# One of four combinations of the down weights on GpSimd instead of VectorE, in a fused convolution and MLP layer

## What is computed

```python
h = rmsnorm(x, mix_norm)
x = x + short_conv_mixer(h, conv_w_in, conv_w, conv_w_out)   # h @ w_in, gates, 3 taps, @ w_out
h = rmsnorm(x, mlp_norm)
a = relu(h @ mlp_w1)
x = x + (a * a) @ mlp_w2                                     # 512x8192 @ 8192x2048
```

## Time and profile before

| | |
|---|---|
| median of 3 runs | 2037.64 us (2037.37 to 2037.85) |
| the profiled execution | 2034.88 us |
| its span | 2033.1 us |
| instructions in it | 22629 |

### The profile page before, as it was taken

One profiled execution on the slowest core, in us unless ns is written; L12 is line 12 of the kernel. 1 busy time (PEld: TensorE's weight loads), 2 busy tenths in 40 slices (PEclk: granted clock), 3 DMA queues, 4 the chain that ended last, 5 costly groups with the idle time before them and its releaser, 6 DMA issues.

```text
span 2033.1 us, 22629 instructions
## 1 busy us (share of the span) xinstructions
PE 2015.3 (99%) x8900; PEld 1665.6 (82%) x8900; DVE 1217.7 (60%) x1362; ACT 657.8 (32%) x876; POOL 30.6 (2%) x62
## 2 busy tenths in 40 slices
PE   8999999999999999999999999999999999999999
PEld 7888888888888888787888888888888888888887
DVE  6345353353543453535364554636988989978878
ACT  6222222222233332323232232323444443333432
POOL 0000000000000000000000000000000000000000
PEclk9999999999999999999999999999999999999999
DMA  5322223222223222536263553639899888888783
GB/s 187 114 93 103 95 91 104 97 88 103 83 104 103 100 87 104 196 118 229 99 248 128 204 198 138 244 108 364 321 359 353 314 336 316 320 316 322 272 316 139
DMA packets 72965, 387.10 MB, mean 190 GB/s; under 512 B 7984, under 2 KB 7984, under 8 KB 41264
## 3 DMA queue, kind: packets, MB, share of 16 engines
q1 hardware_dynamic: 64672, 327.18, 44.3%
q0 software_dynamic: 8064, 58.72, 6.9%
q10 hardware_dynamic: 144, 0.04, 0.0%
HBM read 323.00 MB, written 62.91 MB: 190 GB/s over the span
## 4 chain that ended last, share of the span: by engine, by line
PE 99%; issue 0%; DMA 0%; ACT 0%; DVE 0%; ACTq 0%
PE pair L682 68%; PE pair L781 30%; PE pair L748 0%; DMA cols<-in_cols 0%; PE pair L712 0%; PE pair L705 0%; PE pair L715 0%; PE pair L718 0%; ACT L284 0%; DVE x L601 0%; ACT h_hi L284 0%; ACT w_hi L280 0%; ACTq L340 0%
## 5 line engine op out<-in xcount | busy, mean ns | idle before, releaser
L391 DVE TENSOR_TENSOR w_lo<-w_raw,w_hi 128x512 fp32r<-128x512 f32 x512 | 352.3, 692 | 677.2 <-ACT w_hi L280 671.9
L682 PE MATMUL pair<-h_hi,w_lo 128*128 128x512 f32 x1788 | 698.5, 391 | 6.9 <-issue 6.9
L682 PE MATMUL pair<-h_hi,w_hi 128*128 128x512 f32 x1788 | 695.9, 389 | 0.0
L682 PE MATMUL pair<-h_lo,w_hi 128*128 128x512 f32 x1788 | 695.6, 389 | 0.0
L280 ACT ACTIVATE w_hi<-w_raw 128x512 fp32r<-128x512 f32 x512 | 323.0, 631 | 951.6 <-PE pair L682 949.1
L781 PE MATMUL pair<-d_w,act_hi 128*128 128x512 f32 x1792 | 551.6, 389 | 0.0
L682 PEld LDWEIGHTS pair<-h_hi,w_lo 128*128 128x128 f32 x1788 | 335.6, 188 | 78.2 <-issue 9.5
L781 PEld LDWEIGHTS pair<-d_w,act_hi 128*128 128x128 f32 x1792 | 336.3, 188 | 69.9 <-issue 0.2
L682 PEld LDWEIGHTS pair<-h_hi,w_hi 128*128 128x128 f32 x1788 | 335.6, 188 | 70.2
L682 PEld LDWEIGHTS pair<-h_lo,w_hi 128*128 128x128 f32 x1788 | 335.7, 188 | 69.7 <-issue 0.5
L333 ACT ACTIVATE d_w<-d_raw 128x1024 fp32r<-128x1024 f32 x224 | 233.7, 1059 | 369.6 <-PE pair L781 235.3
(11 more groups left out here) (55 smaller groups left out, 571.9 us busy)
## 6 DMA issues: line engine op xcount, KB each, us to landing
w_raw<-in_weights SPq DMA_DIRECT2D x127, 1024.0 KB, 4.9
d_raw<-in_down SPq DMA_DIRECT2D x64, 1024.0 KB, 8.5
spill<-stage POOLq DMA_DIRECT2D x56, 1024.0 KB, 6.0
act_hi<-spill SPq DMA_DIRECT2D x112, 512.0 KB, 6.5
act_lo<-spill SPq DMA_DIRECT2D x112, 512.0 KB, 7.3
resid<-in_xt SPq DMA_DIRECT2D x3, 1024.0 KB, 12.9
out<-x SPq DMA_DIRECT2D x6, 512.0 KB, 3.3
resid<-in_xt SPq DMA_DIRECT2D x4, 256.0 KB, 6.0
```

Source lines behind the costliest of these rows:

```text
L391: nc.vector.tensor_tensor(w_lo[:, k % RING, :], w_raw[:, k // GRAN % NRAW, k % GRAN, :], w_hi[:, k % RING, :].bitcast(F32), ALU.subtract). ...
L682: mm = nc.tensor.matmul(ps[NT * parity + i], stationary, moving, start=(k == 0 and j == 0), stop=(k == KT - 1 and j == 2))
```

## The change

T3 moves from VectorE to GpSimd. VectorE's order loses it at slot 5. GpSimd, after the spills of the first seven pairs, runs over the 16 units. In each it waits until R12 and R22 have landed and T1 has read R12, then forms T3 and adds one to the new semaphore `t3_formed`. Behind it come the late spills that belong to the unit. ScalarE waits for `t3_formed` in place of `t_formed` before it splits S3's weights (slots 8 and 9). T4 takes number 3, and the counts of `t_formed` go from four to three per unit.

```diff
         MIX, MLP = 0, DT
-        T1, T2, T3, T4 = 1, 2, 3, 4
+        T1, T2, T4, T3 = 1, 2, 3, 4
...
                     if r == R11:
-                        sp.wait_ge(t_formed, 4 * u + T4)
+                        sp.wait_ge(t_formed, 3 * u + T4)
...
-            for c in range(NC):
-                for n, j in enumerate(SPILLS):
-                    pool.wait_ge(stage_lo, NPROD * c + n + 1)
-                    i = (NPROD * c + n) % 2
-                    pool.dma_start(spill[c, j], stage[i][:].bitcast(F32)).then_inc(spilled[i], 16)
+            def put_spill(c, n):
+                pool.wait_ge(stage_lo, NPROD * c + n + 1)
+                i = (NPROD * c + n) % 2
+                pool.dma_start(spill[c, SPILLS[n]], stage[i][:].bitcast(F32)).then_inc(spilled[i], 16)
+
+            for c in range(NC - 1):
+                for n in range(NPROD):
+                    put_spill(c, n)
+            for u in range(NU):
+                pool.wait_ge(d_raw_in[R12], 16 * (u + 1))
+                pool.wait_ge(d_raw_in[R22], 16 * (u + 1))
+                pool.wait_ge(t_formed, 3 * u + T1)
+                nc.gpsimd.tensor_tensor(d_raw[:, R12], d_raw[:, R22], d_raw[:, R12], ALU.subtract).then_inc(t3_formed, 1)
+                for (late_u, _), late in sorted(LATE.items()):
+                    if late_u == u:
+                        put_spill(NC - 1, late[0])
...
-                elif j in (S1, S2, S3, L22):
-                    act.wait_ge(t_formed, 4 * u + {S1: T1, S2: T2, S3: T3, L22: T4}[j])
+                elif j == S3:
+                    act.wait_ge(t3_formed, u + 1)
+                elif j in (S1, S2, L22):
+                    act.wait_ge(t_formed, 3 * u + {S1: T1, S2: T2, L22: T4}[j])
...
             def form_weights(u, t):
-                o, a, b = ((R11, R12, R11), (R11, R22, R11), (R12, R22, R12), (R21, R21, R11))[t - 1]
+                o, a, b = ((R11, R12, R11), (R11, R22, R11), (R21, R21, R11))[t - 1]
...
-                dve.wait_ge(d_lo_ready, SLOTS * u + {T1: 2, T2: 4, T3: 4, T4: 8}[t])
+                dve.wait_ge(d_lo_ready, SLOTS * u + {T1: 2, T2: 4, T4: 8}[t])
                 if t in (T2, T4):
-                    dve.wait_ge(t_formed, 4 * u + {T2: T1, T4: T2}[t])
+                    dve.wait_ge(t_formed, 3 * u + {T2: T1, T4: T2}[t])
...
-                    if s == 5:
-                        form_weights(u, T3)
```

More of the change, by code:

```diff
@@ L152, in conv_mlp_layer @@
         t_formed = sem("t_formed")
+        t3_formed = sem("t3_formed")
         d_hi_ready = sem("d_hi_ready")
```

## The result

The changed kernel takes 2049.4 us in the median of 4 runs (2048.86 to 2051.28). The kernel before has 2037.51 us in its 4 (2035.11 to 2037.85). The ratio is 1.0063, with a 95% interval of 1.0045 to 1.008: slower by 0.6%, clear of the 0.2% that can be told from no change. The forecast was 2050.0 us. Executions of one and the same kernel here lie in two groups some 2 us apart: of 64 of the kernel before, 38 took 2034.51 to 2035.98 us with a mean granted clock of 1.0, and 26 took 2036.89 to 2038.23 us with 0.998 or 0.999.

What follows compares the result with a forecast made beforehand. TensorE was taken to bound the down projection, with VectorE only needing to stay ahead. Ordinary units 9.0 us plus unit 8 3.4 us gave 12.4 us (0.6%), added to the 2037.64 us median: 2050.0 us, range 2037 to 2072.

Steps and rivals of the forecast that it cites:

- What VectorE gives up is worth 0: Down projection: VectorE loses 16 instructions of 2.28 us, 36.5 us in all, worth 0 on TensorE's path.
- T3's length, 4.6 us: GpSimd's two-input T3 of 2048 columns: 4.6 us, the middle between 3.1 and 6.2 us.
- Start 0.2 us after T1, and done long before its user: GpSimd's T3 starts 0.2 us after T1, ready some 9.5 us before ScalarE's split of slot 8; semaphore costs nothing.
- Rival 3: GpSimd gives way to VectorE, T3 gets late for slot 8: 1 us in each of 16 units, 2053; chance 0.04.
- VectorE is held, the addition out of PSUM is not: Behind T1, VectorE's PSUM addition goes on beside T3; slot 2's split, with two SBUF inputs, waits for T3's end.
- D: Delay of slot 2's split on VectorE: 0.2 us + T3's length - 1.14 us, 3.66 us with 4.6.
- rival 1: Slots 2 to 5: engines don't disturb each other (2037.6), or share so the lead holds (half speed 2040.2); chance 0.42.
- Ordinary units, 14 x 0.64 = 9.0 us: Units 1 to 7 and 9 to 15: slot 4 late by 0.54 us, 0.64 with hand-over, 9.0 us in all.
- hand-over: In ordinary units, 0.1 us added to slot 4's 0.54 us lateness, making TensorE's stop 0.64 us.
- Unit 8, 3.4 us: After the sums closing the first half, slot 4's lead is 0.23 us, so TensorE stops 3.66 - 0.23 = 3.4 us.
- Unit 0, nothing: GpSimd's T3 runs 1415.0 to 1419.6, in VectorE's idle stretch before the down projection's first matmul: cost 0.
- R22 lands in time: R22's load for the next unit lands at 1566.1 to 1570.9, ahead of T1's end there at 1571.01.

Runs made afterwards that it cites:

- experiment 1: Kernel before with VectorE's T3 and the wait for it taken out, nothing put in: 2035.38 us against 2035.49, ratio 1.0.
- experiment 3: Changed kernel with GpSimd copying R22 to R12 (one input) in place of T3: 2036.61 us, ratio 1.0004 to the kernel before.
- experiment 2: Changed kernel with GpSimd's T3 replaced by three memsets of the same quarter, so it only writes: 2035.77 us, ratio 1.0002 to the kernel before.
- experiment 9: Changed kernel with GpSimd's T3 waiting in addition for slot 2's split: 2066.88 us, ratio 1.0149 to the kernel before.
- experiment 7: Changed kernel, but VectorE forms T3 in units 0, 7, 8 and 15, GpSimd after slot 5 in the other 12: 2035.58 us against 2035.37.
- experiment 10: Changed kernel, but in unit 8 alone VectorE forms T3 after slot 5: 2044.98 us against 2035.37 for the kernel before, ratio 1.0049.
- experiment 4: Changed kernel with GpSimd forming half of T3's columns, VectorE the rest after slot 5: 2038.52 us, ratio 1.0009 to the kernel before.
- experiment 8: Changed kernel with GpSimd's T3 in two instructions of 1024 columns back to back: 2050.64 us, ratio 1.0063 to the kernel before.
- experiment 5: Changed kernel with GpSimd's T3 waiting in addition for slot 5's split: 2042.76 us, ratio 1.0032 to the kernel before.

## Why the prediction was right

- **What VectorE gives up is worth 0.** Right, shown by experiment 1.
- **T3's length, 4.6 us.** 4.61 us measured. The number was right, its bounds were loose: one input for 2048 columns takes 1.91 us (experiment 3) where 3.1 was worked out from the 128-column select, and two inputs take 2.4 times that, more than the twice that I allowed. The two errors cancel in the middle that I took.
- **Start 0.2 us after T1, and done long before its user.** 0.18 us; no wait of ScalarE for GpSimd in the changed kernel. Rival 3 falls.
- **VectorE is held, the addition out of PSUM is not.** Shown: 5.88 for 2.36 us, beside 1.22 us unchanged. D was forecast as 3.66 us and is 3.52. Experiments 2 and 3 show that it is GpSimd's reading that does it, experiment 9 that the second to begin waits, experiment 7 that a common tile is not needed. So rival 1 falls, in both its forms. T3 took 4.61 us beside a VectorE that wanted to go on, and as much in unit 0, where VectorE was idle until 1419.09, which is no sharing:

```profile
1414.76 4.60 POOL L277 TENSOR_TENSOR d_raw<-d_raw 128x2048 f32<-128x2048 f32 x1 [10.95 <-DVE d_raw L585]
```

The rule of the Trainium skill (SBUF — State Buffer, Who interferes with whom) agrees with each of these measurements. That it is a port that both engines share is the page's explanation; the runs show only who waits for whom.
- **Ordinary units, 14 x 0.64 = 9.0 us.** 0.65 us each (38.73 against 38.08), 9.1 us; with unit 8 taken out the whole kernel loses 9.6 us (experiment 10). Inside the 0.64 us two errors cancel. The delay was 3.52 us and not 3.66, and what I took as 0.1 us of hand-over was 0.65 - (3.52 - 3.12) = 0.25. Unit 8 gives nearly the same in experiment 3, 0.79 - (0.78 - 0.23) = 0.24, and in experiment 4, 1.31 - (1.32 - 0.23) = 0.22.
- **Unit 8, 3.4 us.** Too small, 4.65 us. I counted from slot 4, where the lead is 0.23 us. But TensorE stopped already at slot 2, whose lead in the trace of before is also small: the split ends at 1727.39 + 1.22 = 1728.61 and is due at 1729.28, 0.67 us later.

```profile
1727.39 2.36 DVE L576 TENSOR_TENSOR d_w<-d_raw,d_w 128x1024 fp32r<-128x1024 f32 x2
```

That alone would have given nearly the same, 3.66 - 0.67 = 3.0 us. The term left out, and so put at nothing, is the clock: 1.65 us at the lower level.
- **Unit 0, nothing.** Right: GpSimd works from 1414.76 to 1419.36, VectorE's next instruction is at 1419.09, the first with two SBUF inputs at 1419.81, with its usual 0.69 us.
- **R22 lands in time.** Right by a hair in general, wrong once: in unit 6 GpSimd waited for the load and started 0.6 us after T1's end (T1 ran from 1647.87 to 1650.16). That unit took 39.17 us, 0.4 more than its neighbours. The traces of experiments 8 and 10 have the same wait in the same unit.

```profile
1650.76 4.60 POOL L277 TENSOR_TENSOR d_raw<-d_raw 128x2048 f32<-128x2048 f32 x1 [9.15 <-DMA d_raw<-in_down]
```

The terms come to 9.1 + 4.65 + 0.4 = 14.2 us in the trace. The forecast of 12.4 us had the two last ones too small by 1.7. That its 2050.0 us lies so near to 2049.4 is partly luck: the three executions to which the 12.4 us were added (2037.37 to 2037.85) all belong to the longer group, while the later medians of the kernel before are 2035.4 to 2036.4. Added to those, the forecast would have been 2047.8 to 2048.8.

## What to carry to other kernels

Work moved from VectorE to GpSimd is not beside VectorE's work where GpSimd reads SBUF and VectorE's instruction takes two operands from it (shown here for subtractions in fp32). Count GpSimd's whole length as a delay of VectorE (less what VectorE does meanwhile with an operand in PSUM), and compare it with the lead that the bounding engine has at that very slot, not with VectorE's idle time on average. Look for the units that differ (the first, the last, those with extra sums), for they lose first. If it must be moved, put it where the lead is largest, or beside instructions with an operand in PSUM (the second was not tried by itself). And count what TensorE's clock costs behind a long stop.

## What the runs showed of the hardware

- GpSimd on 128x2048 fp32: memset 1.81 us, copy 1.91, subtraction of two inputs 4.61; 128x1024 with two inputs 2.41.
- A held VectorE instruction is shown as busy and long (T2 with 6.52 us for 2.29), and so is a held GpSimd one (5.41 for 4.61). The list of waits doesn't name it. The mean of a group against that of the kernel before (1458 ns for 1222) gives it away.
- TensorE's clock fell to its lower level after one pause of 2.87 us, in experiment 8 after pauses of 0.70, 0.25 and 1.80 us, and in experiment 9 after one of 4.04 us (unit 8) and after two of 0.95 and 2.44 (unit 0). It did not fall in the ordinary units of the changed kernel, where the loads of weights pause for 0.3 and 0.6 us.
- The same pause can end either way. Each of the twelve traces (the kernel before, the changed one and the ten experiments) has a pause of 2.19 or 2.20 us near 840 us and another near 936 us, in the up projection, which the change does not touch. The clock fell behind 6 of these 24: behind both in experiments 3 and 8, behind the second in experiments 5 and 9. The kernel before, first matmul after the first pause, and the table of stretches behind it:

```profile
842.02 0.47 PE L682 MATMUL pair<-h_hi,w_lo 128*128 128x512 f32 x1 [2.20 <-issue]
...
843.00:847.00 4.00, 4.00 (x19) 3.32 (x18) 1.25 (x2) 0.63 (x1) 0.52 (x1) 1.00 0.98 387
```

The same in experiment 3:

```profile
841.43 0.47 PE L694 MATMUL pair<-h_hi,w_lo 128*128 128x512 f32 x1 [2.20 <-issue]
...
843.00:847.00 4.00, 4.00 (x14) 3.12 (x13) 0.23 (x1) 0.63 (x1) 0.00 (x0) 0.64 1.00 418
```

From this matmul to the first of the down projection there are 577.12 us in the one (842.02 to 1419.14) and 580.35 in the other (841.43 to 1421.78), 3.2 us more for the two stretches. This fits the two groups of executions of the kernel before; that it is their whole cause is not shown, for no execution of the longer group of that kernel was traced. It also means that the 1.65 us of unit 8 are read from one execution and need not be the same in each.
